# Layer ends closed tile by tile, a mixer front and a latent attention in another order, and three first tiles in halves

## What is computed

```python
# first block, layer 0 then 1 (g = norm gains)
h = h + 0.5 * rms_norm(swiglu(rms_norm(h, g[0]), w_in, w_out), g[1])       # f0, f2
m = rwkv7_time_mix(rms_norm(h, g[2]), ...)  or  swa_sinks(rms_norm(h, g[2]), k_sh, v_sh, ...)
h = h + rms_norm(m, g[3])                                                   # mix, swa
h = h + 0.5 * rms_norm(swiglu(rms_norm(h, g[4]), ...), g[5])                # f1, f3
# behind layer 0: k_sh, v_sh = rms_norm(h, kv_norm_g) @ w_kv + b_kv
# second block
h = rmsnorm(x) * (1 + scale) + shift            # shift, scale, gate = c @ w_ada + b_ada
proj = h @ w_in                                 # all inputs of both attentions and the gates
o_a = stick_breaking_attention(...)             # 8 heads
o_b = latent_attention(q, rope(q_pe), k_nope, rope(k_pe), v)   # 8 heads, causal softmax
merged = sigmoid(g_a) * ((o_a*silu(z_a)) @ w_a) + sigmoid(g_b) * ((o_b*silu(z_b)) @ w_b)
out = rmsnorm(x + gate * (merged @ w_out))
```

## Time and profile before

| | us |
|---|---|
| runs | 2800.75, 2803.5, 2810.16 |
| median | 2803.5 |
| the profiled execution: its time | 2804.03 |
| its span, from the first to the last instruction | 2802.2 |
| PE busy | 2670.2 (95%) |
| POOL busy | 1768.9 (63%) |
| DVE busy | 1121.8 (40%) |
| ACT busy | 633.5 (23%) |
| mean granted TensorE clock | 0.978 |

### The profile page before, as it was taken

The page is one execution under the profiler, slowest core; times in us unless marked ns, Lnnn a source line. Parts: engine busy times, 40 slices in busy tenths (PEclk is TensorE's granted clock), DMA queues, the critical chain, the costliest instruction groups (busy, mean ns, idle before and its releaser), DMA issues.

```text
span 2802.2 us, 47886 instructions
## 1 busy us (share of the span) xinstructions
PE 2670.2 (95%) x17904; PEld 2168.6 (77%) x17904; DVE 1121.8 (40%) x1651; ACT 633.5 (23%) x1213; POOL 1768.9 (63%) x1795
## 2 busy tenths in 40 slices
PE   8999998988887999999999999999999999999998
PEld 7888876767775788888888888778888878777677
DVE  3333036874554533310633312775333232123344
ACT  2111025433432211100311101443111011353211
POOL 6777675773321577777577776675777757645565
PEclk9999999989998999999999999999999999999998
DMA  4333322220000233333233332432333323222212
GB/s 138 97 94 97 94 73 71 75 57 4 4 4 16 72 90 94 97 94 98 71 95 97 94 97 84 151 125 70 96 97 94 98 69 103 83 60 72 73 46 79
DMA packets 116792, 225.94 MB, mean 81 GB/s; under 512 B 13088, under 2 KB 13856, under 8 KB 115616
## 3 DMA queue, kind: packets, MB, share of 16 engines
q1 hardware_dynamic: 114624, 209.46, 25.9%
q10 hardware_dynamic: 2016, 14.22, 1.4%
HBM read 221.53 MB, written 2.10 MB: 80 GB/s over the span
## 4 chain that ended last, share of the span: by engine, by line
PE 84%; DVE 9%; ACT 3%; issue 2%; POOL 1%; DMA 1%; SPq 0%; DVEq 0%; ACTq 0%; POOLq 0%
PE bank L222 21%; PE bank L224 21%; PE bank L223 21%; PE bank L326 1%; DVE acc L322 1%; PE bank L1330 1%; DVE h L705 1%; PE bank L1862 1%; PE bank L240 1%; PE bank L241 1%; PE bank L244 1%; DVE x_lo L1090 1%; PE bank L1345 1%; PE bank L2296 1%; PE bank L2287 1%
## 5 line engine op out<-in xcount | busy, mean ns | idle before, releaser
L209 POOL TENSOR_TENSOR w_lo<-w_raw,w_hi 128x512 fp32r<-128x512 f32 x778 | 1046.8, 1345 | 761.6 <-PE bank L224 613.3
L222 PE MATMUL bank<-x_hi,w_hi 128*128 128x512 f32 x1904 | 752.5, 395 | 12.6 <-issue 5.3
L224 PE MATMUL bank<-x_hi,w_lo 128*128 128x512 f32 x1904 | 749.5, 394 | 0.0
L223 PE MATMUL bank<-x_lo,w_hi 128*128 128x512 f32 x1904 | 748.0, 393 | 0.0
L214 POOL TENSOR_SCALAR w_hi<-w_raw 128x512 fp32r<-128x512 f32 x778 | 579.3, 745 | 4.9 <-DMA w_raw<-weights 4.9
L222 PEld LDWEIGHTS bank<-x_hi,w_hi 128*128 128x128 f32 x1904 | 359.4, 189 | 98.9 <-issue 9.0
L223 PEld LDWEIGHTS bank<-x_lo,w_hi 128*128 128x128 f32 x1904 | 359.6, 189 | 78.6 <-issue 0.2
L224 PEld LDWEIGHTS bank<-x_hi,w_lo 128*128 128x128 f32 x1904 | 359.3, 189 | 77.9
L670 DVE TENSOR_TENSOR f<-bank,rstd 128x512 f32<-128x512 f32 x88 | 56.7, 686 | 596.6 <-PE bank L224 589.0
L224 PE MATMUL bank<-mid_hi,w_lo 128*128 128x512 f32 x704 | 276.0, 392 | 0.0
L223 PE MATMUL bank<-mid_lo,w_hi 128*128 128x512 f32 x704 | 275.6, 392 | 0.0
(11 more groups left out here) (438 smaller groups left out, 3513.3 us busy)
## 6 DMA issues: line engine op xcount, KB each, us to landing
w_raw<-weights SPq DMA_DIRECT2D x778, 256.0 KB, 2.6
ada_w<-ada_in ACTq DMA_DIRECT2D x8, 1536.0 KB, 7.1
h<-xT SPq DMA_DIRECT2D x4, 512.0 KB, 7.1
out<-f SPq DMA_DIRECT2D x8, 256.0 KB, 2.2
mask_b<-mask_b_in ACTq DMA_DIRECT2D x1, 640.0 KB, 4.9
spread<-spread_in SPq DMA_DIRECT2D x1, 512.0 KB, 8.0
window<-window_in ACTq DMA_DIRECT2D x1, 512.0 KB, 3.7
masks<-masks_in SPq DMA_DIRECT2D x1, 320.0 KB, 7.8
```

Source lines behind the costliest of these rows:

```text
L209: pool.tensor_tensor(w_lo[:, (n - 1) % RW, :], w_raw[:, (n - 1) % RS, :], w_hi[:, (n - 1) % RW, :].bitcast(F32), ALU.subtract).then_inc(w_ ...
L222: pe.matmul(outs[m], w_hi[:, s, c], hi, start=first, stop=False)
L223: pe.matmul(outs[m], w_hi[:, s, c], lo, start=False, stop=False)
L224: done = pe.matmul(outs[m], w_lo[:, s, c], hi, start=False, stop=last)
```

## The change

- **Layer ends, all six** (f0, mix, f1, f2, swa, f3): `closing_products` does the last three units of the last half output tile by output tile, nine matmuls for each, and tells `out_ready` tile by tile and `w_used` only within the last tile. Norm.post has `(7,)`: tile 6 goes to DVE's `acc`.
- **Halves:** behind mix, f2 and swa the first tile of f, h and `x_hi` is done in two halves of 256 columns, with semaphores `f_half`, `h_half`, `x_half`; PE does its hi products in two rounds of eight half matmuls.
- **Mixer front:** the wide inverse norm goes to SETA's bank 3; the first two u tiles read it there. `keys_early` does keys b=0 with the hi products ahead of `x_lo`. Four buffers for the mixed tiles below q=8. Low-rank inputs in another order and the last two behind tile 7. k 4 to 7 are copied out ahead of tiles 14 and 15. The low-rank units 2 and 3 are split by output tiles. `v_out(0)` stands inside factors(5). `r_gather` stands behind `blank(pool, 0)`.
- **Swa end, f3 front:** ada products of two columns each (three, then eight places), with one unread matmul of 128 columns each in the swa end; two per k for k<7 in f3's front.
- **Latent attention:** unit order gates(1), keys(0), queries(1), keys(1), v; scores(0), (1), (2) stand among them; ACT copies v out behind exp(1); the branch units of b=0 stand in rounds 9 to 11, in bank sets of three and one.

```diff
+        CLOSING = 3
+        def closing_products(pe, outs, hi, lo, n0, tiles):
+            ks = range(tiles - CLOSING, tiles)
+            for m, o in enumerate(outs):
+                c = slice(m * P, (m + 1) * P)
+                for k in ks:
+                    if m == 0:
+                        pe.wait_ge(w_lo_ready, n0 + k + 1)
+                    w = (n0 + k) % RW
+                    pe.matmul(o, w_hi[:, w, c], hi[:, k, :], start=False, stop=False)
+                    pe.matmul(o, w_hi[:, w, c], lo[:, k, :], start=False, stop=False)
+                    done = pe.matmul(o, w_lo[:, w, c], hi[:, k, :], start=False, stop=k == tiles - 1)
+                    if m == len(outs) - 1:
+                        done.then_inc(w_used, 1)
+                    elif k == tiles - 1:
+                        done.then_inc(out_ready, 1)
...
+        def early_products(pe, outs, k, x0, n, halved=0):
...
+            for t, ready in ((slice(0, T // 2), (x_half, halved)), (slice(T // 2, T), (x_hi_ready, x0 + 1))) if halved and k == 0 else \
+                    ((slice(0, T), (x_hi_ready, x0 + k + 1)),):
+                pe.wait_ge(*ready)
+                for m, o in enumerate(outs):
...
-                self.pre, self.post = Norm(KT, ODD), Norm(KT, (6, 7), late=True)
+                self.pre, self.post = Norm(KT, ODD), Norm(KT, (7,), late=True)
+                self.halved = {1: 1, 3: 3}.get(number, 0)
...
+        def halves_of_first(dve, s, number):
+            dve.wait_ge(wide_ready, s.post.index + 1)
+            dve.wait_ge(f_ready, s.h0 // 2 + 1)
+            for t, scaled_, added in ((slice(0, T // 2), f_half, h_half), (slice(T // 2, T), tmp_ready, h_ready)):
...
+        def mix_at(q):
+            return sq[:, q % 2, :] if q % 4 < 2 or q >= KT else (acc, sq_last)[q % 2][:]
...
+            for k in each:
+                keys_early(k)
+            pe.wait_ge(*rv("back", 1))
...
+            pe.wait_ge(*ra("k", 3))
+            low_rank(0, range(4)).then_inc(w_used, 1)
+            pe.wait_ge(*ra("k", 7))
+            low_rank(1, range(4)).then_inc(w_used, 1)
...
+            pe.wait_ge(*ra("sg", 3))
+            low_rank(2, (1, 2, 3))
+            pe.wait_ge(*ra("sg", 6))
+            low_rank(3, (0, 1, 2))
+            pe.wait_ge(*ra("norm"))
+            low_rank(2, (0,)).then_inc(w_used, 1)
+            pe.wait_ge(*ra("sg", 7))
+            low_rank(3, (3,)).then_inc(w_used, 1)
...
+            factors(5, lambda: v_out(0))
...
-            ada_products(pe, 1, 4)
+            ada_products(pe, 0, 2, unread=True)
             norm_wide(pe, s.post, bank[s.post_at][1])
-            ada_products(pe, 4, 12)
+            ada_products(pe, 2, 10, unread=True)
...
+            latent_keys(pe, s, 0, sb_)
+            pe.wait_ge(*pa("gb1", 3))
+            latent_queries(pe, s, 1, sa)
...
-            pe.wait_ge(*lv("v", TT - 1))
+            pe.wait_ge(*lv("k", 3))
             pe.wait_ge(*la("k"))
+            scores(0)
+            pe.wait_ge(*lv("q", 7))
+            latent_keys(pe, s, 1, bank[SETA])
+            scores(1)
+            pe.wait_ge(*lv("k", 7))
+            for k in range(2):
+                moving_units(pe, bank[SETA], ckv_hi, ckv_lo, k, 2, s.n_uv + k)
+            scores(2)
+            pe.wait_ge(*la("v", TT - 1))
...
+                if i >= HEADS_B + 1:
+                    for k in ((0,), (1, 2), (3,))[i - HEADS_B - 1]:
+                        branch_unit(pe, s, 0, k)
+        BRANCH = (bank[SETB][0:3] + bank[SETA][3:], bank[SETA][0:3] + bank[SETB][3:])
...
+                if i == 1:
+                    act.wait_ge(w_used, s.n_uv + 2)
+                    act.wait_ge(rinv_ready, s.kv.index + 1)
+                    for t in range(TT):
+                        act.activation(mla_v[:, t, :], bank[SETA][t][:], ACT.Copy, scale=rinv[:, t:t + 1]).then_inc(*la.tell("v", t))
...
-            pool.wait_ge(*lv("v", TT - 1))
+            pool.wait_ge(w_used, s.n_a)
```

More of the change, by code:

```diff
@@ L865, in rwkv_tensor @@
-            pe.wait_ge(*rv("wa_lo"))
-            for j, free in enumerate((ra("k", 3), ra("k", 7), ra("norm"), ra("sg", 7))):
-                if j == 2:
-                    pe.wait_ge(*ra("sg", 0))
-                    for k in each:
-                        g = slice(32 * (k % 4), 32 * (k % 4) + 32)
-                        done = pe.matmul(sa[0][g, :], gather[:, k, :], square_of(k), start=k < 4, stop=k >= 4, skip_group_check=True)
-                    done.then_inc(*rp.tell("sums"))
-                pe.wait_ge(*free)
-                unit_products(pe, [o[:] for o in bank[(SETA, SETB)[j % 2]]], wa_hi[:], wa_lo[:], True, True, s.n_lora2 + j)
+            norm_wide(pe, s.pre, sa[3])
@@ new lines, in keys_early @@
+            def keys_early(k):
+                n = s.n_k + k
+                pe.wait_ge(w_lo_ready, n + 1)
+                pe.wait_ge(x_hi_ready, s.x0 + k + 1)
+                for m in range(4):
+                    if k == 0 and m == 3:
+                        pe.wait_ge(rstd_ready, s.rs + 1)
+                    c = slice(m * P, (m + 1) * P)
+                    pe.matmul(sa[m][:], w_hi[:, n % RW, c], x_hi[:, k, :], start=k == 0, stop=False)
+                    pe.matmul(sa[m][:], w_lo[:, n % RW, c], x_hi[:, k, :], start=False, stop=False)
+                pe.wait_ge(x_lo_ready, s.x0 + k + 1)
+                for m in range(4):
+                    done = pe.matmul(sa[m][:], w_hi[:, n % RW, m * P:(m + 1) * P], x_lo[:, k, :], start=False, stop=k == KT - 1)
+                done.then_inc(w_used, 1)
@@ new lines, in rwkv_tensor @@
+            pe.wait_ge(*ra("k", 7))
+            low_rank(1, range(4)).then_inc(w_used, 1)
+            pe.wait_ge(*ra("sg", 0))
+            for k in each:
+                g = slice(32 * (k % 4), 32 * (k % 4) + 32)
+                done = pe.matmul(sa[0][g, :], gather[:, k, :], square_of(k), start=k < 4, stop=k >= 4, skip_group_check=True)
+            done.then_inc(*rp.tell("sums"))
+            pe.wait_ge(*ra("sg", 3))
+            low_rank(2, (1, 2, 3))
+            pe.wait_ge(*ra("sg", 6))
@@ L945, in tile @@
                     mix(q + 1)
-                act.wait_ge(mixed, q + 1)
-                if q >= KT:
-                    act.wait_ge(w_used, x_free(s, q))
-                act.activation(x_hi[:, q % KT, :], sq[:, q % 2, :], ACT.Copy).then_inc(x_hi_ready, 1)
+                high(q)
             mix(0)
-            act.wait_ge(u_ready, 1)
-            act.activation(rstd[:], bank[SETA][1][:], ACT.Copy).then_inc(rstd_ready, 1)
-            for q in each:
-                tile(q)
+            act.wait_ge(u_ready, 2)
+            act.activation(rstd[:], bank[SETA][3][:], ACT.Copy).then_inc(rstd_ready, 1)
+            high(0)
+            mix(1)
+            for q in range(1, KT):
+                mix(q + 1)
+                high(q)
             act.wait_ge(*rv("in", 0))
@@ L973, in rwkv_scalar @@
                 norm_square(m)
-            for q in range(KT, 2 * KT):
+            for q in range(KT, 2 * KT - 2):
                 tile(q)
@@ L2696, in _ @@
             blank(pool, 0)
+            for k in each:
+                pool.tensor_scalar(r_gather[:, k, :], gather[:, k, 0:HEADS], vcol("r_k", k), None, ALU.mult).then_inc(*rg.tell("gather", k))
             with pool.Fori(0, (core_at - mix.n_k) // RW - ahead) as i:
```

230 lines of the change are left out of this document (128 added, 102 removed).

## The result

The changed kernel takes 2784.79 us (median of four, 2782.1 to 2790.69) against 2805.13 beside it: a ratio of 0.993, 95% interval 0.9906 to 0.9954. Run again with the experiments it took 2784.04 (six, 2777.35 to 2789.47) against 2806.15, ratio 0.9915 (0.9899 to 0.9932). So it is faster by 0.7 to 0.85%, 20 to 24 us; the intervals alone allow 13 to 28. Its first profiled execution took 2790.69 us, with a span of 2788.8.

A forecast was written before the change was run, and what follows sets the result against it. PE, busy 2670.2 of 2802.2 us, was taken as the bound, so only its waits, half clock and filler could be won. Terms for layer ends, mixer, swa end and latent attention sum to 17.3; forecast 2786 us, range 2774 to 2797.

The forecast's parts named there:

- Latent attention: From query unit 1 to the branch units: score groups between units cover PE's idle time; +8.9 us, 5 if at half clock.
- The mixer: Mixer front to core start: earlier first key unit and low-rank work; core start taken as +6 us (3 to 10).
- the 5.0 at R: In the mixer, R, behind the low-rank work and ACT's sixteen sigmoids, was to start 5.0 us earlier (4.3 to 5.5).
- f0's end: Layer end f0: POOL is behind, PE stalls 2.1 us, the root still comes 0.6 earlier; net +0.8 us (0 to 2).
- Plain ends: Ends of mix, f1, f2: root net 0.9 us earlier, 0 to 0.8 given back beside splits; +0.5, +0.6, +0.5.
- The halves: First tiles behind mix, f2 and swa: first x_hi some 0.3 us earlier, costed at nothing; -0.3 to +0.5 each.
- Swa end: End of swa: PE stalls 2.9 us in the closing, root 0.3 earlier, half clock left as is; net +1 (-3 to +3).
- f3's end: Layer end f3: root +0.9 us, but two or three of DVE's product steps meet a split; net -1 (-1.5 to +0.5).
- A: Rival: the shared port takes the mixer's gain; mixer gives 1 us, the ends nothing; 2793 us, chance 0.20.
- B: Rival: more gain; core start takes 10 us, the swa end's half-clock stretch shortens by 3; 2778 us, chance 0.17.
- C: Rival: closings at layer ends wait for w_lo, a mean cost of 2.9 us an end; 2812 us, chance 0.05.
- D: Rival: in latent attention late k and q copies move the waits, half the gain stays; 2791 us, chance 0.10.

## Why the prediction was right, point by point

**The total.** 2786 was said and 2784.8 measured, in the range and on the side forecast. The gain by the stretches is 17.8 against 17.3, but that is partly luck: the swa end brought 2.8 more than said, and latent attention (1.0), the ends of mix and f2 (1.1) and the mixer (0.5) brought as much less. The start of the sum is a little off too: a unit takes 2.75 us in a quiet stretch, not 2.73.

**Latent attention** (8.9; measured 7.9). The working holds to the step: turned scores 7.0 earlier in the first profile where 7.25 was said, POOL's turn the next thing late, the mask's transfer hidden. Where the new stretch is at full clock the gain is 8.6. The rest is the half-clock stretch at 2637.8, which some profiles have (120.5) and some not (119.0); it stood as the lower bound.

**The mixer** (6.8 for both rows; measured 6.3). At the core's start the number is less good. Counted from split 124 to the inverse, the old code takes 258.6 and 261.2 us, the changed one 253.0 to 256.9, 4.4 less in the mean, where 6.8 was said; from split 176 on it is 1.2 longer, where 1 shorter was said. The other 1.8 us come behind the inverse, in the core, where the sum has nothing and the stretches at half clock scatter: that the row comes out is luck. The working itself adds up to 5.5 (5.0 + 1.3 + 0.7 - 1.5), of which 6 was made. The idle time before the first key product went from 5.29 to 3.19, as said (2.2). Two steps of the way were wrong; the second explains the 2.4 that are missing at the core's start. First, x_lo(7) was put at 449.9 to 451 from a start at 423.75, about 26.7 us on; the start came later (427.38) and the end at 450.2, 22.8 us on, where the old order takes 28.3. So the steps between were mis-sized by 4 us, and f0's end (below) hid it; of these the two more buffers, which were to "free only ACT", hold about 2 (24.8 with two of them, one profile). Second, the 5.4 us of waiting for `v_arr` were called "hidden behind DVE anyway", and r_gather was to cost DVE 1 to 2: DVE did end at 603.6, better than said, but V's products ended at 605.5 and held the core. The price of r_gather is on PE's side, 4.37 of waiting, and it is worth 2.7 at the core. The wait of 3.67 for `k_arr` became 3.73 for the first sigmoids, which the 5.0 at R had in it.

**f0's end** (+0.8). The stall, 1.97 for 2.1, is right. It was followed by half clock inside the closing in eight of nine profiles that have the closing and the late columns, 1.6 us that the sum had not: the root's reciprocal stands 33.5 behind split 124 (31.9 in the ninth, that without halves), where the old end has 32.4, 33.4 and 34.1. From there to the second root's the changed front takes 35.9 (seven of these nine; 34.6 and 35.4 in the others), the old one 33.1 and 34.3. DVE has the same steps to do there and is busy for 28.5 to 28.9 us instead of 24.0: POOL's folded splits come beside its steps and cost about 2, the upper end of my 1 to 2. And taking r_gather out of that place gave nothing (34.2 with the old end and r_gather gone): its wait of 1.44 was not on the path that sets the end, DVE's chain was. With r_gather gone the next splits move up beside DVE's steps, and DVE is busy 27.1 us there instead of 24.0. The second root came some 2 us later, where 0.8 earlier was said.

**Plain ends** (0.6). In f1 the working holds to the step: the root stands 2.2 behind the last product (2.3 said), and counted from split 340 it comes 0.91 sooner (0.9 said):

```profile
1327.44 1.00 PE L347 MATMUL bank<-ones,acc 128*128 128x64 f32 x8
1328.28 1.06 PE L347 MATMUL bank<-ones,sq_last 128*128 128x64 f32 x8
...
1329.43 0.26 ACT L374 ACTIVATE root<-bank,eps 128x4 f32<-128x4 f32 x1 [0.84 <-PE bank L347]
...
1331.88 0.94 DVE L749 TENSOR_TENSOR h<-h,f 128x512 f32<-128x512 f32 x1
```

and the add meets the last split by 0.25. **The halves** were costed at nothing and cost 0.6 to 0.7 each behind mix and f2, beyond the -0.3 of the bound. They made the first product come 1.0 sooner, not 0.3. The step that failed is that an earlier first unit frees a weight slot, so that a split comes sooner; I followed DVE and PE and not the releaser of POOL.

**Swa end** (+1; measured 3.8). The waits in the closing, 1.06 and 1.41, add up to 2.5 (2.9 said), but the half clock of before, 6.7 us of loss in the earlier trace rows, was left "as it is", with the note that the stall would be just ahead of it. It went. That term was mis-sized by its whole uncertainty. The larger part of why the clock stayed is open. **f3's end** (-1) came at -0.8 (-1.3 without the one high old value) by the steps named: 1.55 lost beside the splits, 0.9 gained at the root.

**The rivals.** A is out: the mixer kept 4.4 us at the core's start, where A had 1. It is right in kind, as most of what was lost or not won (halves, f3, f0, the preparation with r_gather moved) is the shared port. B had half its cause right, the clock at the swa end. C did not decide: the waits in closings were 2.0 and 2.5 us in two ends and a few tenths elsewhere, far from a mean cost of 2.9 an end. D is out.

## What to carry to other kernels

When a change lets PE release a buffer earlier, follow the release to the engine that refills it, and look at which operation of a third engine the refill will meet: here that alone turned a gain of 0.6 us into nothing at two ends. Small side work of POOL is best put beside products in a steady stretch with spare time, not into the gap where everybody waits. And measure a gain of a us by marks that both traces have, stretch by stretch, since the total of one and the same kernel scatters by 12 us over six executions (2777.35 to 2789.47).

## What the runs showed of the hardware

The half-clock stretches move from one execution to the next of the same code: the same latent stretch takes 119.0 us without one and 120.5 with 3.4 us of half clock in it. They do not explain the scatter of the totals: the two profiles of the changed kernel have spans of 2788.8 and 2784.8, and the shorter one has no less half clock (mean granted clock 0.980 in both). The r_gather operations of 128x16 took 0.33 us each beside products alone, 4.10 for eight beside the mixer's first front and 6.56 beside DVE's preparation: very small POOL operations are longer beside DVE's too.

And a full clock can go with a longer time, in the one profile that has it here. In the kernel with latent attention alone f3's old end and the front behind it ran at full clock throughout, in the kernel before 6.8 us of it at half (2301.4 to 2308.2). The adds of the one at full clock:

```profile
2314.93 1.78 DVE L705 TENSOR_TENSOR h<-h,f 128x512 f32<-128x512 f32 x1
...
2319.28 1.09 DVE L705 TENSOR_TENSOR h<-h,f 128x512 f32<-128x512 f32 x1
2323.18 1.10 DVE L705 TENSOR_TENSOR h<-h,f 128x512 f32<-128x512 f32 x1
2326.91 1.10 DVE L705 TENSOR_TENSOR h<-h,f 128x512 f32<-128x512 f32 x1
```

Compared with the kernel before, its first split in the front comes 2.4 us sooner, and from the fourth add on every add meets a split: a unit takes 3.7 to 3.9 us there and not 2.7 to 2.9, and the stretch 62.4 us and not 59.5. In the kernel before only two adds are slowed (1.79 and 1.10), then the two engines run past each other.
